# Sorting the rows for the experts by native fp32 products, in two halves with the first experts between them

## The chip, the cores and the metric

The kernel runs on one core of a Trainium2 chip, as one launch. The core has five engines: PE (TensorE, products), DVE (VectorE), ACT (ScalarE), POOL (GpSimd) and SP (SyncE, which here only issues transfers), and 16 DMA engines. They run their own instruction streams and meet at semaphores. The metric is the device time of one execution in microseconds, lower is better.

## The reference

One layer of a hybrid decoder for a prompt of 256 tokens and 8 sequences of 8 tokens, 320 rows of 1024 in all: two attention-like branches, a merge, and a mixture of experts. The change lies in the last part:

```python
t = rmsnorm(x, norm2_g)                       # 320 rows x 1024
g_idx = top-1 of 4 groups;  e_idx, e_p = top-2 of the 8 experts of that group
for each of 32 experts e (w_gate, w_up: 1024 x 256, w_down: 256 x 1024):
    h = silu(t @ w_gate[e]) * (t @ w_up[e])   # for the rows that chose e
    out += (h * combine[:, e]) @ w_down[e]
y = x + out
```

Each row chooses two experts, so there are 640 pairs (slots). All is float32. The weights of the experts are 96 arrays of 1 MB.

## The kernel before, in words

Each engine has one block of code with its instructions in a fixed order; nothing is scheduled by a program. In the order of time:

- The dense part: 48 chunks of weights of 1 MB (`w_dense`), each split by ACT and DVE into a rounded high and a low half (type fp32r, tensor `rm`), and multiplied by PE.
- The router: x1 (the rows after the merge) is scaled to h2 by ACT (L1041). PE makes the logits, and a long chain of small DVE instructions (L1516 to L1547) finds each row's two experts and with them its two places among the 640 slots, sorted by expert.
- The sort: DVE writes a one-hot matrix `onehot` (320 rows in 3 tiles, 640 columns; L1551, L1552), and PE multiplies h2 by it, so that the result `xs` has each slot's row as a column, slots in the order of experts. fp32r products are exact only for rounded data, so h2 goes in as a high part (ACT, L1042) and a low one (POOL, L694, h2 minus the high part). There are 16 pieces (8 blocks of 128 features, two halves of 320 slots) of 5 products each (L2023), in the banks 0 to 3, taken to `xs` by ACT (L1053) and DVE (L1564).
- The experts: POOL (ACT for expert 0) copies the 64 slots from where an expert's begin into `pack`; `gate_up` makes 16 products for gate and up (L2042, L2044), ACT and DVE make `hact`, PE transposes it (L2053), and `down` (L2062) multiplies it by the third array. `start(v + 1)` stands ahead of `down` of v, with v's transposes in its middle. The results go out to `y_rows` by an indirect DMA from POOL (L714). The table of rows that this needs (`rows_ready`) comes from 6 small products (L2081) behind expert 0's gate and up. An expert with more than 64 rows would send all through another path (`crowd`), which isn't taken with these inputs.
- At the end SP reads back x1 and the rows, DVE adds them (L1641), and SP writes y.

The 96 arrays are numbered in the order of use: 0 and 1 are gate and up of expert 0, 2 and 3 those of expert 1, 4 is down of 0, 5 and 6 gate and up of 2, and so on (`unit`). They go through 21 slots of 1 MB, array n in slot n mod 21. SP issues them in this order (L455), and each wait holds all behind it. Waits: 4 and 5 for the dense part's last sections, 6 for the merge's splits, 9 and 10 for the last two chunks to be split, 11 for PE's last dense product, 14 for POOL's subtractions (`h2_split`), 17 for the whole sort (`sorted_full`), and from 21 on for `e_used`, which PE raises twice at the end of `gate_up` and once at the end of `down`.

Of the kernel before, what the change touches and what calls it, by code (L numbers as in the profile page):

```python
# [157 lines left out]
def hybrid_step(nc, A, O):  # L158
# [10 lines left out]
    with ctx:  # L169
# [80 lines left out]
        for i in range(2):  # L250
# [41 lines left out]
        top[0] = base_att  # L292
# [22 lines left out]
        top[0] = base_yrow  # L315
# [10 lines left out]
        assert top[0] <= FW  # L326
        squares, lgT = em[:, 12288 + 384:12288 + 384 + CW], em[:, 12288 + 640:13312]
        turn40 = fm[:, base_masks + 1240:base_masks + 1280]
        blkf = cube(fm[:, base_rt:base_rt + NE * JB], NE)

        top[0] = base_raw + 5 * UN
        xe = cube(take(3 * D), 3)
        gat = [take(D) for _ in range(6)]
        crowd_s = [take(D)[0:NS, :] for _ in range(2)]
        assert top[0] <= base_yrow
# [4 lines left out]
                for i in range(2)]  # L340
# [7 lines left out]
        slot = rawm[8:12] + [halves[8192], halves[8192 + UN], rawm[2], rawm[3], rawm[4], rawm[0], rawm[1],  # L348
                             halves[13312], halves[13312 + UN], halves[13312 + 2 * UN]] + rawm[5:8] + \
                            [halves[q * UN] for q in range(4)]  # L350
        NEARLY = 4
        NSLOT = len(slot)
        pack = [cube(em[:, 12288 + 512 * i:12288 + 512 * (i + 1)], KC) for i in range(2)]
        h2s = [cube(rm[:, 3072 * i:3072 * (i + 1)], 3) for i in range(2)]
        onehot = cube(rm[:, 6144:6144 + 3 * SLOTS], 3)
# [52 lines left out]

        def weights(v, j):

            n = unit(v, j)
            return slot[n % NSLOT]
# [24 lines left out]
        def _(sp):  # L437
# [14 lines left out]
            def load(n):  # L452

                v, j = order[n]
                sp.dma_start(slot[n % NSLOT], A["w_moe"][3 * v + j]).then_inc(landed(v, j)[0], 16)  # L455
# [26 lines left out]
            for n in range(NEARLY, 3 * NE):  # L482
                if n == 4:

                    sp.wait_ge(sem("unit_full"), units(first("out"))[0])
                elif n == 6:

                    sp.wait_ge(sem("m_split"), KC)
                    sp.wait_ge(sem("samp_hi"), 1 + KC)
                elif n in (9, 10):  # L490

                    sp.wait_ge(sem("split_done"), NCH - 1 + n - 9)
                elif n == 11:

                    sp.wait_ge(sem("unit_full"), sum(units(NCH - 1)))
                elif n == 14:

                    sp.wait_ge(sem("h2T_full"), 2 * CPS)
                    sp.wait_ge(sem("h2_split"), 3)
                elif n == 17:  # L500

                    sp.wait_ge(sem("sorted_full"), 2 * KC)
                elif n >= NSLOT:

                    sp.wait_ge(sem("e_used"), n - NSLOT + 1 if n < 3 * NE - 1 else unit(NE - 8, 2) + 1)
                load(n)

            sp.wait_ge(sem("e_used"), 3 * NE - NSLOT + 4)
# [38 lines left out]
        def _(pool):  # L547
# [143 lines left out]
            for t in range(3):  # L691
                r = ROWS[t]
                pool.wait_ge(sem("h2_hi"), t + 1)
                g(nc.gpsimd.tensor_tensor(h2s[1][:, t, :] if t < 2 else h2s[0][NS:2 * NS, t, :], h2[0:r, t, :],  # L694
                                          h2s[0][0:r, t, :], ALU.subtract), sem("h2_split"))

            def packed(v):

                place = pool.value_load(off_i[:, v:v + 1], min_val=0, max_val=SLOTS)
                if v >= 2:  # L700

                    pool.wait_ge(sem("e_used"), unit(v - 2, 1) + 1)
                nc.gpsimd.tensor_copy(pack[v % 2], xs[:, :, bass.ds(place, CAP)]).then_inc(sem("e_packed"), 1)
# [56 lines left out]
        def _(act):  # L760
# [278 lines left out]
            for t in range(3):  # L1039
                r = ROWS[t]  # L1040
                s(A_(h2[0:r, t, :], h2[0:r, t, :], ACT.Copy, scale=small[0:r, 9 + t:10 + t]))  # L1041
                s(A_(h2s[0][0:r, t, :], h2[0:r, t, :], ACT.Copy), sem("h2_hi"))  # L1042
# [7 lines left out]
            for n in range(0, 2 * KC, 2):  # L1050
                k, half = n // 2, n % 2
                act.wait_ge(sem("sorted_full"), n + 1)
                s(A_(xs[:, k, NT * half:NT * (half + 1)], bank[n % 4][:, 0:NT], ACT.Copy), sem("sorted_free_a"))  # L1053
# [8 lines left out]
            act.wait_ge(sem("sorted_free_v"), KC)  # L1062
            A_(pack[0], xs[:, :, 0:CAP], ACT.Copy).then_inc(sem("e_packed"), 1)
            for v in range(NE):

                act.wait_ge(sem("e_used"), unit(v, 1) + 1)
                A_(act_g[v % 2][CAP:2 * CAP, :], bank[v % 2][0:CAP, 0:FE], ACT.Silu).then_inc(sem("e_silu"), 1)  # L1067
                if v >= 1:
                    take_y(v - 1)
            take_y(NE - 1)  # L1070
# [13 lines left out]
        def _(dve):  # L1084
# [464 lines left out]
            s(CP(place[NS:2 * NS, 2, :], place[0:NS, 2, :]))  # L1549
            for t in range(3):  # L1550
                s(TSC(onehot[:, t, :], iota, place[:, t, 0:1], None, ALU.is_equal))  # L1551
                s(STT(onehot[:, t, :], iota, place[:, t, 1:2], onehot[:, t, :], ALU.is_equal, ALU.add),  # L1552
                  sem("onehot"))
# [4 lines left out]
            s(v.tensor_reduce(most[:, 0:1], bank[4][:, 0:NE], AX_X, ALU.max))  # L1558
            dve.wait_ge(sem("x1_stored"), 16)
            s(v.memset(xs[:, :, SLOTS:XC], 0.0))  # L1560
            for n in range(1, 2 * KC, 2):
                k, half = n // 2, n % 2
                dve.wait_ge(sem("sorted_full"), n + 1)
                s(CP(xs[:, k, NT * half:NT * (half + 1)], bank[n % 4][:, 0:NT]), sem("sorted_free_v"))  # L1564
            dve.wait_ge(sem("sorted_free_a"), KC)
            s(v.memset(small[0:1, 94:95], 0.0), sem("xs_ready"))

            for k in range(2):
                s(TT(esel, hot[k], offs.unsqueeze(1).broadcast_to([P, 3, NE]), ALU.mult))
                s(v.tensor_reduce(scal[3 * k + 1], esel, AX_X, ALU.add))  # L1570
                s(TT(scal[3 * k], place[:, :, k], scal[3 * k + 1], ALU.subtract))
                for t in range(3):
                    i, r = 3 * k + t, ROWS[t]
                    s(TSC(at_rank[i][0:r, :], iota[0:r, 0:CAP], scal[3 * k][0:r, t:t + 1], row_of[0:r, i:i + 1],
                          ALU.is_equal, ALU.mult), sem("onehot"))
            dve.wait_ge(sem("router_full"), 6)
            s(TSC(row_i, bank[6][0:CAP, 0:NE], float(NO_ROW), None, ALU.add), sem("rows_ready"))

            def late_words():

                dve.wait_ge(sem("router_exps"), 1)
                s(v.tensor_reduce(wsum, gexp, AX_X, ALU.add))
                s(TSC(wden, second, 1.0, None, ALU.add))
                s(TT(wsum, wsum, wden, ALU.mult))
                s(v.reciprocal(wts[:, :, 0], wsum))
                s(TT(wts[:, :, 1], wts[:, :, 0], second, ALU.mult))
                crowd3 = crowd_i.rearrange("p (t k) -> p t k", t=3)
                for k in range(2):
                    s(STT(crowd3[:, :, k], picks[:, :, k], float(JB * CAP), scal[3 * k], ALU.mult, ALU.add))
                s(CP(flag_i, most[0:1, 0:1]))  # L1590
                for j in range(JB):
                    s(TSC(blkf[0:1, :, j], offs[0:1, :], float(CAP * j), float(SLOTS), ALU.add, ALU.min))
                s(CP(blk_i, blkf[0:1, :, :].rearrange("p e j -> p (e j)")))
# [8 lines left out]
            for e in range(NE):  # L1602
# [4 lines left out]
                if e == 0:  # L1607
                    late_words()
                if e >= 1:
                    take_y(e - 1)  # L1610
                dve.wait_ge(sem("e_hT_full"), e + 1)
                CP(htp[e % 2], cube(bank[2 + e % 2][:, 0:2 * CAP], 2)).then_inc(sem("e_hT"), 1)  # L1612
            take_y(NE - 1)
# [32 lines left out]
        def _(pe):  # L1646
# [372 lines left out]
            def sort(n, t):  # L2019

                k, half = n // 2, n % 2
                for i in range(2 if t < 2 else 1):
                    ins = mm(bank[n % 4][:, 0:NT], h2s[i][:, t, P * k:P * (k + 1)],  # L2023
                             onehot[:, t, NT * half:NT * (half + 1)], start=(t == 0 and i == 0), stop=(t == 2))
# [3 lines left out]
            for t in range(3):  # L2028
                pe.wait_ge(sem("h2_split"), t + 1)
                pe.wait_ge(sem("onehot"), t + 1)  # L2030
                for n in range(4):
                    sort(n, t)
            for n in range(4, 2 * KC):
                pe.wait_ge(sem(("sorted_free_a", "sorted_free_v")[n % 2]), n // 2 - 1)
                for t in range(3):
                    sort(n, t)
# [38 lines left out]

            start(0)
            pe.wait_ge(sem("onehot"), 3 + 6)
            for k in range(2):
                for t in range(3):
                    i, r = 3 * k + t, ROWS[t]  # L2080
                    ins = mm(bank[6][0:CAP, 0:NE], at_rank[i][0:r, :], hot[k][0:r, t, :], start=(i == 0), stop=(i == 5))  # L2081
            ins.then_inc(sem("router_full"), 1)
            for v in range(NE):
# [14 lines left out]
                down(4 + v % 2, htp[v % 2], weights(v, 2)).then_inc(sem("e_used"), 1)  # L2098

# [84 lines left out]
```

## Time and profile before

| what | value |
|---|---|
| three executions | 875.36, 878.8, 879.83 us (median 878.8) |
| the profiled execution | 872.89 us, its span 871.4 us, mean granted clock of PE 0.949 |
| PE busy | 750.2 us, 86% |
| PE's weight loads busy | 597.2 us, 69% |
| DVE busy | 401.8 us, 46% |
| ACT busy | 298.5 us, 34% |
| POOL busy | 144.1 us, 17% |
| DMA | 202.84 MB, mean 233 GB/s |

Busy shares are means over stages that differ. The part at hand begins at about 600 us, where the dense part ends, and goes to the end of the span. A row of a timeline gives start, length, engine, line, operation, operands and the count of instructions merged in it; in square brackets stands how long the engine was idle before it and what ended that. A row of windows gives a stretch, its length, the busy time and instructions of each engine, PE's granted clock (1 is 2.4 GHz, 0.5 is 1.2 GHz), the busy share of the DMA engines and their GB/s.

### The profile page before, as it was taken

The numbers are of one execution on the slowest core, as the hardware profiler recorded it, in microseconds if no ns is written. First come the engines' busy times: TensorE is split into PE (matmuls) and PEld (weight loads), VectorE is DVE, ScalarE is ACT, GpSimd is POOL, SyncE is SP. The second block draws the span as 40 slices with busy tenths as digits, with TensorE's granted clock in tenths as the row PEclk, the third lists the DMA queues.
The fourth block names the chain that finished last, engine by engine and source line by source line (L and its number), as shares of the span: only waits on it lengthen the run. The fifth ranks groups of instructions, "written<-read, shape, count | busy, mean of one in ns | idle before, by whom it ended". The sixth has DMA issues, their size and how long they took to land.

```text
span 871.4 us, 14531 instructions
## 1 busy us (share of the span) xinstructions
PE 750.2 (86%) x5476; PEld 597.2 (69%) x5476; DVE 401.8 (46%) x936; ACT 298.5 (34%) x550; POOL 144.1 (17%) x245
## 2 busy tenths in 40 slices
PE   2999899998888999997968799986589999787780
PEld 1899899996555699996857689985555555444440
DVE  3575333466544456584445547764752222111123
ACT  5433553655333255663221224544221111111110
POOL 5001000002333200103222300001212222112210
PEclk9999999999899999999989999998699999999995
DMA  5245233226677642727565625984579999999986
GB/s 184 97 146 181 101 142 139 104 97 213 173 232 219 194 146 103 255 97 237 140 206 168 191 93 189 347 344 171 224 318 418 417 419 418 419 418 419 418 322 190
DMA packets 38170, 202.84 MB, mean 233 GB/s; under 512 B 7490, under 2 KB 8018, under 8 KB 18898
## 3 DMA queue, kind: packets, MB, share of 16 engines
q1 hardware_dynamic: 24434, 160.29, 48.1%
q0 software_dynamic: 13664, 41.58, 15.3%
q8 instruction: 46, 0.75, 0.4%
q14 instruction: 26, 0.21, 0.1%
HBM read 184.24 MB, written 23.38 MB: 238 GB/s over the span
## 4 chain that ended last, share of the span: by engine, by line
PE 59%; DMA 17%; DVE 11%; ACT 5%; issue 5%; SPq 1%; POOLq 1%; POOL 1%; DVEq 0%; ACTq 0%
PE bank L1694 20%; PE bank L1698 9%; DMA fm<-in_w_moe 7%; DMA em<-in_w_moe 7%; PE bank L2042 6%; PE bank L1684 3%; PE bank L1850 3%; PE bank L2062 3%; DMA fm<-in_cache_lf 2%; DVE rm L1104 2%; PE bank L1899 2%; ACT rm L781 2%; PE bank L2023 2%; PE bank L1839 1%; PE bank L1934 1%
## 5 line engine op out<-in xcount | busy, mean ns | idle before, releaser
L1694 PE MATMUL bank<-rm 128*128 128x320 f32 x1344 | 207.5, 313 | 2.6 <-ACT fm L809 1.6
L1694 PEld LDWEIGHTS bank<-rm 128*128 128x128 f32 x1344 | 199.0, 189 | 7.4 <-issue 3.9
L1104 DVE TENSOR_TENSOR rm<-fm,rm 128x2048 fp32r<-128x2048 f32 x48 | 110.0, 2293 | 69.5 <-ACT rm L781 69.0
L1698 PE MATMUL bank<-rm 128*128 128x256 f32 x960 | 122.4, 286 | 2.4 <-DVE fm L1474 2.4
L1698 PEld LDWEIGHTS bank<-rm 128*128 128x128 f32 x960 | 118.4, 194 | 3.2 <-issue 2.9
L2044 PE MATMUL bank<-fm,em 128*64 128x256 f32 x384 | 98.1, 401 | 0.0
L781 ACT ACTIVATE rm<-fm 128x2048 fp32r<-128x2048 f32 x48 | 91.9, 1915 | 17.8 <-PE bank L1694 11.2
L2042 PE MATMUL bank<-em 128*64 128x256 f32 x272 | 66.7, 389 | 9.8 <-DMA fm<-in_w_moe 6.4
L2042 PE MATMUL bank<-fm,em 128*64 128x256 f32 x240 | 61.7, 404 | 12.2 <-DMA fm<-in_w_moe 10.8
L2042 PEld LDWEIGHTS bank<-em 128*64 128x64 f32 x272 | 35.6, 138 | 36.5 <-issue 21.9
L1067 ACT ACTIVATE fm<-bank 64x256 f32<-64x256 f32 x32 | 12.0, 376 | 136.3 <-PE bank L2044 136.3
L2042 PEld LDWEIGHTS bank<-fm,em 128*64 128x64 f32 x240 | 32.6, 143 | 36.3 <-issue 21.8
L714 POOL DMA_INDIRECT y_rows<-fm,im x32 | 29.3, 915 | 161.5 <-DVE fm L1600 150.5
L2044 PEld LDWEIGHTS bank<-fm,em 128*64 128x64 f32 x384 | 51.7, 142 | 0.0
L1316 DVE SCALAR_TENSOR_TENSOR fm<-fm,bank 128x257 f32<-128x257 f32 x64 | 28.0, 479 | 48.1 <-PE bank L1850 48.1
L648 POOL DMA_DIRECT2D fm<-in_state_C x32 | 17.7, 552 | 178.2 <-DVE fm L1257 118.7
L1684 PE MATMUL bank<-rm 128*128 128x256 f32 x320 | 43.1, 287 | 0.6 <-DVE fm L1445 0.6
L1605 DVE TENSOR_TENSOR fm<-bank,fm 64x256 f32<-64x256 f32 x32 | 13.6, 426 | 63.6 <-ACT fm L1067 63.3
L1684 PEld LDWEIGHTS bank<-rm 128*128 128x128 f32 x320 | 40.0, 191 | 2.8 <-DVE fm L1474 1.5
L1612 DVE COPY fm<-bank 128x128 f32<-128x128 f32 x32 | 9.3, 292 | 66.3 <-PE bank L2053 51.5
L1850 PE MATMUL bank<-fm 64*128 64x257 f32 x128 | 29.6, 471 | 8.1 <-ACT fm L929 7.1
L1600 DVE COPY fm<-bank 64x512 f32<-64x512 f32 x32 | 22.2, 694 | 29.4 <-PE bank L2062 29.4
(387 smaller groups left out, 1013.3 us busy)
## 6 DMA issues: line engine op xcount, KB each, us to landing
fm<-in_w_moe SPq DMA_DIRECT2D x57, 1024.0 KB, 27.6
fm<-in_w_dense SPq DMA_DIRECT2D x48, 1024.0 KB, 4.9
em<-in_w_moe SPq DMA_DIRECT2D x39, 1024.0 KB, 27.7
fm<-in_state_C POOLq DMA_DIRECT2D x32, 257.0 KB, 4.4
out_C_sample<-fm POOLq DMA_DIRECT2D x32, 257.0 KB, 5.3
fm<-in_cache_kT POOLq DMA_DIRECT2D x16, 512.0 KB, 5.0
fm<-in_cache_v POOLq DMA_DIRECT2D x16, 512.0 KB, 4.5
fm<-y_rows SPq DMA_DIRECT2D x4, 512.0 KB, 5.3
```

The lines of the kernel that those rows point to most:

```text
L714: pool.indirect_dma_start(y_rows, bass.IndirectOffsetOnAxis(ap=row_i[:, v:v + 1].bitcast(U32), axis=0), yrow[v % NY], None, bounds_check=6 ...
L781: s(A_(pair[c % 2][0], cube(raw[c % RAW1], KC), ACT.Copy), sem("hi_done"))
L1104: s(TT(pair[c % 2][1], cube(raw[c % RAW1], KC), pair[c % 2][0], ALU.subtract), sem("split_done"))
L1316: done(STT(Cout[n % NCOUT][:, k, :], Cin[n % NCIN][:, k, :], dec8[:, HM * b + h:HM * b + h + 1], bank[bk][:, 0:DE], ALU.mult, ALU.add), bk)
L1600: CP(yrow[v % NY][:, D // 2:D], bank[4 + v % 2][CAP:2 * CAP, :]).then_inc(sem("e_y_right"), 1)
L1684: ins = mm(bank[b][:, 0:CW], samp[:, k, :], w[:, k, :], start=(k == 0 and i == 0), stop=(k == KC - 1 and i == 1))
L1694: ins = mm(bank[b][:, 0:NT], w[:, k, P * u:P * (u + 1)], a[:, k, :], start=first, stop=final)
L1698: ins = mm(bank[b][0:r, 0:CW], a[:, k, TILE0[u]:TILE0[u] + r], w[:, k, :], start=first, stop=final)
L1850: full(mm(bank[bk][:, 0:DE], kwm[n % 2][rows, 0:P], vx2[rows, h, :], start=True, stop=True), bk)
L2042: last_g = mm(bank[b][0:CAP, 0:FE], x[:, k, :], g[:, k, :], start=(k == 0), stop=(k == KC - 1), skip_group_check=True)
L2044: last_u = mm(bank[b][CAP:2 * CAP, 0:FE], x[:, k, :], u[:, k, :], start=(k == 0), stop=(k == KC - 1), skip_group_check=True)
L2062: ins = mm(bank[b][CAP * j:CAP * (j + 1), :], hT[:, k, :], w[:, k, 512 * j:512 * (j + 1)], start=(k == 0), stop=(k == 1), skip_group_check ...
```

## The change

- h2 is sorted as it is: the sort's products take h2 and `onehot` in float32, one product for a tile instead of two. ACT's rounded copy and POOL's subtraction are gone, and PE waits for the scaling alone (`h2_scaled`).
- The slots are sorted in two halves of 320. The first half (8 pieces of 3 products) is done ahead of expert 0. The first five experts can't reach beyond slot 320 (5 x 64; the starts of 1 to 4 are limited to that), so the second half comes later: 4 pieces behind down of expert 1 and 4 behind down of expert 2, in the banks 6 and 7. POOL waits for it ahead of expert 5's pack.
- DVE writes the first half's one-hot columns for the three tiles ahead of the sort, the second's between its evacuations. The table of rows is made behind down of expert 0, some small words later than before.
- Since `rm` holds neither h2's parts nor `onehot`, and h2 lies elsewhere, 18 arrays (0 to 17) have a slot ahead of the sort. 18 to 25 go into the slots of 0 to 7 again, each once its array is used. 26, 27 and 28 take the last three slots, which hold h2 and `onehot` until then, and wait for the whole sort.

```diff
-        slot = rawm[8:12] + [halves[8192], halves[8192 + UN], rawm[2], rawm[3], rawm[4], rawm[0], rawm[1], ...
+        slot = rawm[8:12] + [halves[8192], halves[8192 + UN]] + rawm[2:6] + [rawm[0], rawm[1], halves[13312], ...
...
+        NSLOT, NFREE, NAGAIN = len(slot), 18, 8
+        HALF, NBEFORE = SLOTS // 2, 5
-        h2s = [cube(rm[:, 3072 * i:3072 * (i + 1)], 3) for i in range(2)]
-        onehot = cube(rm[:, 6144:6144 + 3 * SLOTS], 3)
+        onehot = cube(em[:, 0:3 * SLOTS], 3)
...
+        def slot_of(n):
+            if n < NFREE:
+                return n
+            if n < NFREE + NAGAIN:
+                return n - NFREE
+            return n - NAGAIN if n < NSLOT + NAGAIN else slot_of(n - NSLOT)
...
-                elif n in (9, 10):
-                    sp.wait_ge(sem("split_done"), NCH - 1 + n - 9)
-                elif n == 11:
+                elif n in (10, 11):
+                    sp.wait_ge(sem("split_done"), NCH - 1 + n - 10)
+                elif n == 12:
                     sp.wait_ge(sem("unit_full"), sum(units(NCH - 1)))
-                elif n == 14:
-                    sp.wait_ge(sem("h2T_full"), 2 * CPS)
-                    sp.wait_ge(sem("h2_split"), 3)
-                elif n == 17:
+                elif n == NFREE + NAGAIN:
                     sp.wait_ge(sem("sorted_full"), 2 * KC)
-                elif n >= NSLOT:
+                    sp.wait_ge(sem("late_done"), 1)
+                elif NFREE <= n < NFREE + NAGAIN:
+                    sp.wait_ge(sem("e_used"), n - NFREE + 1)
+                elif n >= NSLOT + NAGAIN:
                     sp.wait_ge(sem("e_used"), n - NSLOT + 1 ...
...
-            for t in range(3):
-                r = ROWS[t]
-                pool.wait_ge(sem("h2_hi"), t + 1)
-                g(nc.gpsimd.tensor_tensor(h2s[1][:, t, :] ..., h2[0:r, t, :], h2s[0][0:r, t, :], ALU.subtract), sem("h2_split"))
             def packed(v):
                 place = pool.value_load(off_i[:, v:v + 1], min_val=0, max_val=SLOTS)
+                if v == NBEFORE:
+                    pool.wait_ge(sem("xs_ready"), 2)
...
+            def hot_slots(t, half):
+                w, r = slice(HALF * half, HALF * (half + 1)), ROWS[t]
+                s(TSC(onehot[0:r, t, w], iota[0:r, w], place[0:r, t, 0:1], None, ALU.is_equal))
+                s(STT(onehot[0:r, t, w], iota[0:r, w], place[0:r, t, 1:2], onehot[0:r, t, w], ALU.is_equal, ALU.add), sem("onehot"))
...
-            def sort(n, t):
-                k, half = n // 2, n % 2
-                for i in range(2 if t < 2 else 1):
-                    ins = mm(bank[n % 4][:, 0:NT], h2s[i][:, t, P * k:P * (k + 1)], onehot[:, t, NT * half:NT * (half + 1)], ...)
+            def sort(b, k, half, t):
+                r = ROWS[t]
+                ins = mm(bank[b][:, 0:HALF], h2[0:r, t, P * k:P * (k + 1)], onehot[0:r, t, HALF * half:HALF * (half + 1)], ...)
...
                 down(4 + v % 2, htp[v % 2], weights(v, 2)).then_inc(sem("e_used"), 1)
+                if v == 0:
+                    row_table()
+                elif v in (1, 2):
+                    sort_more(range(4 * (v - 1), 4 * v))
```

On SP, the issues of the experts' arrays from number 6 on, before (`em` and `fm` are the two tensors that hold the slots; a count at the end is of equal rows):

```order
L455 DMA fm<-in_w_moe 128x2048 [waits samp_hi,m_split]
L455 DMA fm<-in_w_moe 128x2048 x2
L455 DMA fm<-in_w_moe 128x2048 [waits split_done] x2
L455 DMA em<-in_w_moe 128x2048 [waits unit_full]
L455 DMA em<-in_w_moe 128x2048 x2
L455 DMA fm<-in_w_moe 128x2048 [waits h2_split,h2T_full]
L455 DMA fm<-in_w_moe 128x2048 x2
L455 DMA em<-in_w_moe 128x2048 [waits sorted_full]
L455 DMA em<-in_w_moe 128x2048 x3
L455 DMA fm<-in_w_moe 128x2048 [waits e_used] x4
```

and now:

```order
L462 DMA fm<-in_w_moe 128x2048 [waits samp_hi,m_split]
L462 DMA fm<-in_w_moe 128x2048 x3
L462 DMA fm<-in_w_moe 128x2048 [waits split_done] x2
L462 DMA em<-in_w_moe 128x2048 [waits unit_full]
L462 DMA em<-in_w_moe 128x2048 x5
L462 DMA fm<-in_w_moe 128x2048 [waits e_used] x4
L462 DMA em<-in_w_moe 128x2048 [waits e_used] x2
L462 DMA fm<-in_w_moe 128x2048 [waits e_used] x2
L462 DMA fm<-in_w_moe 128x2048 [waits late_done,sorted_full]
L462 DMA em<-in_w_moe 128x2048
L462 DMA fm<-in_w_moe 128x2048
```

The issues behind the last dense product are six instead of three, the three behind POOL's subtractions are gone, eight that wait for e_used come next, and the wait for the sort stands ahead of number 26 instead of 17.

On PE, the part from down of expert 0 to the start of expert 3, now (L2080 and L2082 are gate and up, L2091 the transposes, L2100 down, L2120 the table of rows, L2052 the sort):

```order
L2100 MATMUL bank<-em,fm 64x512 [waits e_hT,e_down_in0]
L2100 MATMUL bank<-em,fm 64x512 x3
L2120 MATMUL bank<-fm 64x32 [waits onehot]
L2120 MATMUL bank<-fm 64x32 x5
L2080 MATMUL bank<-em 64x256 [waits e_gate_up_in2,e_hact,e_packed]
...
L2100 MATMUL bank<-fm 64x512 [waits e_hT,e_down_in1]
L2100 MATMUL bank<-fm 64x512 x3
L2052 MATMUL bank<-em,fm 128x320 [waits onehot]
L2052 MATMUL bank<-em,fm 128x320 x5
L2052 MATMUL bank<-em,fm 128x320 [waits sorted_free_a]
L2052 MATMUL bank<-em,fm 128x320 x2
```

Before, no product of the sort stood behind the first expert; the sort began and ended like this:

```order
L2016 MATMUL bank<-rm 128x32
L2023 MATMUL bank<-rm 128x320 [waits onehot,h2_split]
L2023 MATMUL bank<-rm 128x320 x7
...
L2023 MATMUL bank<-rm 128x320 [waits sorted_free_v]
L2023 MATMUL bank<-rm 128x320 x4
L2042 MATMUL bank<-fm,em 64x256 [waits e_gate_up_in0,e_packed]
```

The same 12 products as behind expert 1 stand behind down of expert 2.

## Rows read from the trace of the kernel before

**Rows 1.** Windows, all engines, behind the sort's start; columns as said above.
```profile
624.00:636.00 12.00, 11.32 (x73) 10.79 (x71) 5.32 (x13) 3.50 (x8) 0.00 (x0) 0.96 0.00 0
640.00:740.00 100.00, 98.03 (x744) 52.95 (x742) 28.06 (x71) 16.81 (x35) 25.49 (x34) 1.00 1.01 418
740.00:840.00 100.00, 80.64 (x538) 41.86 (x534) 18.35 (x39) 12.56 (x26) 19.80 (x26) 0.93 1.01 418
```

**Rows 2.** The chain of waits at the end: start, us, what.
```profile
811.52 29.02 DMA fm<-in_w_moe
...
867.31 0.75 DVE fm L1641
```

**Rows 3.** DMA issues of the page: count, size of one, median us to landing.
```profile
fm<-in_w_moe SPq DMA_DIRECT2D x57, 1024.0 KB, 27.6
```

**Rows 4.** Timeline of SP's issues of experts' arrays.
```profile
565.59 20.52 SPq L455 DMA_DIRECT2D fm<-in_w_moe  x5
600.24 1.28 SPq L455 DMA_DIRECT2D em<-in_w_moe  x3
614.56 1.28 SPq L455 DMA_DIRECT2D fm<-in_w_moe  x3
635.52 1.99 SPq L455 DMA_DIRECT2D em<-in_w_moe  x4
640.56 5.83 SPq L455 DMA_DIRECT2D fm<-in_w_moe  x4
```

**Rows 5.** Timeline of POOL and DVE in the router.
```profile
607.25 7.22 POOL L694 TENSOR_TENSOR rm<-fm,rm 128x1024 fp32r<-128x1024 f32 x3 [4.42 <-ACT rm L1042]
...
608.36 1.28 DVE L1522 CAST fm<-im 128x24 f32<-128x24 uint32 x1
...
609.87 2.24 DVE L1528 SCALAR_TENSOR_TENSOR fm<-fm 128x32 f32<-128x32 f32 x1
...
612.67 1.85 DVE L1528 SCALAR_TENSOR_TENSOR fm<-fm 128x32 f32<-128x32 f32 x1
...
615.08 0.19 DVE L1528 SCALAR_TENSOR_TENSOR fm<-fm 128x32 f32<-128x32 f32 x1
...
615.84 0.18 DVE L1533 CAST fm<-im 128x24 f32<-128x24 uint32 x1
```

**Rows 6.** Timeline of the one-hot columns (DVE) and of the sort (PE).
```profile
619.93 0.55 DVE L1551 TENSOR_SCALAR rm<-fm 128x640 fp32r<-128x640 f32 x1
620.52 0.88 DVE L1552 SCALAR_TENSOR_TENSOR rm<-fm,rm 128x640 fp32r<-128x640 f32 x1
...
621.55 4.70 PE L2023 MATMUL bank<-rm 128*128 128x320 f32 x20 [1.90 <-DVE rm L1552]
...
626.42 9.07 PE L2023 MATMUL bank<-rm 128*128 128x320 f32 x60 [0.17 <-ACT fm L1053]
```

**Rows 7.** Windows of PE alone: stretch, length, busy, granted clock, DMA share, GB/s.
```profile
624.00:625.00 1.00, 1.00 (x6) 0.53 0.00 0
625.00:626.00 1.00, 1.00 (x9) 1.00 0.00 0
```

**Rows 8.** Timeline of native fp32 products of full shape in the dense part.
```profile
149.41 0.59 PE L1807 MATMUL bank<-fm 128*128 128x257 f32 x2
149.63 0.84 PEld L1811 LDWEIGHTS bank<-fm 128*128 128x128 f32 x4
...
149.84 1.03 PE L1811 MATMUL bank<-fm 128*128 128x257 f32 x4
```

**Rows 9.** The chain of waits in the first experts: start, us, what.
```profile
640.53 1.02 PE bank L2081 x12
...
650.59 0.26 PE bank L2053 x2
...
656.17 0.27 PE bank L2053 x2
```

**Rows 10.** Timeline of POOL: the pack of expert 2.
```profile
642.56 0.61 POOL L703 COPY em<-fm 128x512 f32 x1 [4.32 <-DVE im L1577]
```

## What I predict, before the changed kernel has run

> **What bounds the kernel now.** I read the windows first, in stretches around the expert part. From 640 to 740 us and from 740 to 840 us the 16 DMA engines are busy all the time and move 418 GB/s, while TensorE has 98 and then 81 of 100 us; from 624 to 636 us nothing moves at all [rows 1]. So behind the sort the weights of the experts are the bound, and before it there is an idle stretch in which they could have come. The chain of waits says the same from the other end: its last long piece is a weight transfer that lands at 840.54 us, and behind it lies a tail of two experts, the last rows and the output, up to 871.4 us [rows 2]. The tail is not touched.
>
> The rest is a count of transfers. One is 1024 KB [rows 3], so at 418 GB/s it takes 2.51 us; there are 96. SP's issues show when they may start: 11, 12 and 13 (counted from 0) at 600.24 us, 14 to 16 at 614.56, when POOL has the last low half, 17 to 20 at 635.52, when the sort is over, and from 21 on as slots come free, from 640.56 [rows 4]. Thus 17 of 96 have come before 635.52, and 79 follow without a gap: 79 x 2.51 = 198 us, and the 7 us left up to 840.5 are for the rows written meanwhile. **Whatever the change does between 600 and 840 us, the end moves by the idle time of DMA that it adds or takes.**
>
> **The change, part by part.**
> *POOL's subtractions go.* Between 607.25 and 614.47 us POOL subtracts three times (2.4 us each). In the same stretch three of DVE's router instructions take 1.28, 2.24 and 1.85 us; the next of the same forms, with POOL idle, take 0.18 and 0.19 [rows 5]. The last long one ends at 614.52 us and POOL's last at 614.47, the first at 609.64 and POOL's first, at a third of its 7.22 us, at 609.66. I take it that they wait for POOL, and that the chain through the router loses (1.28 - 0.18) + (2.24 - 0.19) + (1.85 - 0.19) = 4.8 us. If the three are long for another reason, nothing is won; bounds 0 and 4.8. ACT's three rounded copies (L1042) go as well, which no one waits for any longer.
>
> *The one-hot columns come in halves, and a copy ahead of them goes.* One tile is 0.55 + 0.88 us of DVE for 640 columns [rows 6]; half of it is 0.72, so 0.7 earlier, and the copy at L1549 is 0.2. TensorE began at 621.55; now 621.55 - 4.8 - 0.7 - 0.2 = 615.8. The second halves lie between the evacuations, whose partner TensorE is 1.6 us per bank away, so I cost them at nothing; without that cover they are 2.2 us.
>
> *80 rounded products become 24, and 24 more later.* Before, 20 products took 4.9 us and 60 took 9.1, the first at a granted clock of about 0.5, which is 1.2 GHz [rows 6, 7]. A native product of 320 columns isn't in the trace. The nearest rows: at L1807 and L1811 a product of 257 columns of the same full shape starts 0.43 us after the one ahead, at the full clock [rows 8]. By columns, 320 / 257 x 0.43 = 0.54 us, and 1.07 at 1.2 GHz. Bounds: 0.151 us (what a rounded one of 320 costs, 9.07 / 60) and 0.75 (0.54 and a weight load of 0.21 that isn't hidden). I take 0.54. The clock rose at some 624.94 us (0.53 over 624 to 625, then 1.00), 3.4 us after the dense work began [rows 7]; with that, 3.2 products by 619.2, and 20.8 x 0.54 = 11.2 behind, so the first half ends at **630.4** (before, all of it at 635.5). DVE has x1_stored to wait for; x1 and the first three transfers at 600.24 shared the engines before, as they do now, and its first use is at some 622 us, so nothing.
>
> *From the first half to the end of the second.* From the end of the sort to the end of expert 0's gate and up it was 640.56 - 635.52 = 5.0 us. A further expert is 656.17 - 650.59 = 5.58 us of TensorE [rows 9]. The table of rows is 1.02. It now stands behind down(0), and POOL packs expert 2 only once rows_ready is there: the copy began 642.56 - 641.55 = 1.0 us after the table and takes 0.61 [rows 9, 10], so TensorE stands 1.6 us, where before that lay beside expert 1. Then expert 2's gate and up, down(1), 12 products (6.44), expert 3's and down(2), 12 products. Sum: 5.0 + 5.58 + 1.02 + 1.62 + 5.58 + 6.44 + 5.58 + 6.44 = 37.3 us, so the second half ends at **667.7**. DVE's late words stand behind its copy for down(1) and are covered by the products; before, down(0) waited for them.
>
> *The transfers.* Number 9 needs no end of splitting and is issued with 6 to 8 while the queue is full; 12 to 17 all go at 600.24. They and x1's 1.5 MB are 19 us of DMA, so 18 have come by some 621, when it goes idle. Numbers 18 to 25 each wait for e_used, the first at 630.4 + 5.0 = 635.4 instead of 635.5 for four at once, the last when down(1) ends at 649.3. They need 8 x 2.51 = 20.1 us and have come at **656**. Number 26 waits for the whole sort, 667.7, and SP's queue stands behind it: 12 us idle in the middle of the stretch that sets the end. Then 70 are left.
>
> *Sum.* Before, 79 from 635.5; now 70 from 667.7: 667.7 - 635.5 - 9 x 2.51 = 32.2 - 22.6 = **+9.6 us**. TensorE isn't the bound instead: 28 experts x 5.58 from 667.7 are done at 824, transfers at 850. Against the profiled execution (872.9, span 871.4) that is 882.5; this execution is the fastest of those shown, and on the median of 878.8 it is **888.4 us**.
>
> **A rule against the rows.** The rows show a weight load of 0.21 us for this kind of data (0.84 for four at L1811) and products 0.43 us apart with it, so it is hidden behind 257 columns [rows 8]. The Trainium skill, TensorE: Matmul & The Clock Gate, section "Weight-path perf modes — Fast Weight Load (FWL) and DoubleRow", says that the fast way of loading weights is off for fp32 input. If its cost came out beside the product, each of the 48 would be dearer by the row's 0.21: that is the fourth rival.
>
> **The rivals.**
> 1. *Not slower: the second half is in place before the 26th transfer is asked for, so DMA never idles there.* For it: the rounded product of 320 columns costs 0.151 us. The end moves by 44.8 products (20.8 and 24), so it decides where the second half ends at 658.1, which is a native product of 0.54 - 9.6 / 44.8 = 0.33 us. At 0.27, half of mine, it ends at 655.6 and the change is 655.6 - 658.1 = -2.5 us: 876.3. Against it: 0.43 us for 257 columns, wherever the trace has them.
> 2. *POOL does not hold DVE.* The 4.8 us stay: 893.2. For it: only three of some fifteen instructions there are long. Against: their ends.
> 3. *The clock stays at 1.2 GHz through the first half*, since only 24 products of one kind stand there behind an idle router: 24 x 1.07 = 25.7 instead of 14.6, so 899.5. Against: it rose in 3.4 us before, in the same place.
> 4. *Weight loads beside the products*: 44.8 x 0.21 = 9.4 us, 897.8.
>
> **How the numbers follow.** Forecast 0.68, rival 1 0.12, rival 2 0.11, rivals 3 and 4 together 0.09. The forecast's own range is 882 to 893: 1.6 less if POOL's wait is hidden, 1.7 either way for the clock's rise, and 2.5 either way for how the three runs lie about their median (875.4 to 879.8). With rival 2 above and part of 1 below, 881 to 897. What can be told from no change here is about 0.5%, 4.4 us: slower is above 883.2, faster below 874.4. Rival 1 gives 0.04 to faster and 0.08 to no change; of the forecast 0.04 falls to no change. Faster 0.04, same 0.12, slower 0.84.
>
> **What would show it.** SP's issue of number 26 some 12 us after number 25's transfer has landed, with DMA share 0 between; two idle stretches of DMA (about 621 to 636, 656 to 668) where there was one of 12 us; DVE's L1528 (now L1537) at 0.19 us; native products 0.54 us apart; a gap of about 1.6 us on TensorE ahead of expert 2; the last weights landing at about 850 us of a profile, the tail 31 us as before. I am wrong if issue 26 comes before 658 us, if products are under 0.33 us, or if DMA has a share under 1 behind 668 us, which would mean that it isn't the bound there.

## The result and the profile after

| | executions | median us | lowest to highest |
|---|---|---|---|
| before | 4 | 879.32 | 875.36 to 880.95 |
| after | 4 | **891.87** | 890.79 to 895.51 |

The ratio is 1.0157, with a 95% interval of 1.0112 to 1.0202: slower by 1.6%. I had said 888.4 us, in a range of 881 to 897. The profiled execution of after took 892.09 us, its span is 890.6 us at a mean granted clock of 0.948. That is 19.2 us over the span of before, while the medians are 12.6 us apart; this is taken up below.

In SP's issues of the experts' arrays (start, us, engine, line, operation, operands, count) of after

```profile
567.89 20.54 SPq L462 DMA_DIRECT2D fm<-in_w_moe  x6
602.56 2.98 SPq L462 DMA_DIRECT2D em<-in_w_moe  x6
640.79 4.67 SPq L462 DMA_DIRECT2D fm<-in_w_moe  x4
646.39 7.02 SPq L462 DMA_DIRECT2D em<-in_w_moe  x2
653.45 23.47 SPq L462 DMA_DIRECT2D fm<-in_w_moe  x3
676.97 0.43 SPq L462 DMA_DIRECT2D em<-in_w_moe  x1
```

12 to 17 go together at 602.56 us, 2.3 us later than the same moment of before [rows 4]. This offset comes from the dense part, whose work the change leaves as it is. What makes it is open: that moment lies between 600.2 and 602.0 us in the three profiles of kernels built on before, and between 602.4 and 604.5 in the eight of kernels built on after. Number 18 is asked for at 640.79. The row at 653.45 is the one to learn from: three issues in 23.47 us. 24 and 25 went at its start, the third is number 26, which stood at the head of SP's queue until the sort was over at 676.57, and went at 676.59 (its issue is the last 0.33 us of the row).

The windows (stretch, length, then busy time of PE, PEld, DVE, ACT and POOL, granted clock, DMA share, GB/s) show what the 16 engines did meanwhile, against one idle stretch of some 12 us in before [rows 1]:

```profile
620.00:624.00 4.00, 4.00 (x10) 2.54 (x9) 0.74 (x4) 0.00 (x0) 0.00 (x0) 0.59 0.98 412
625.50:641.70 16.20, 14.83 (x76) 8.18 (x77) 9.36 (x25) 4.04 (x7) 0.61 (x1) 1.00 0.00 0
642.00:665.00 23.00, 21.38 (x130) 11.11 (x128) 5.60 (x19) 2.81 (x6) 3.75 (x5) 1.00 0.90 366
665.00:671.60 6.60, 6.60 (x34) 3.15 (x34) 1.39 (x3) 1.40 (x3) 0.90 (x1) 1.00 0.01 2
672.30:677.60 5.30, 5.30 (x23) 2.72 (x24) 1.25 (x3) 0.44 (x1) 0.00 (x0) 1.00 0.03 5
680.00:740.00 60.00, 60.00 (x452) 31.86 (x448) 15.23 (x32) 10.63 (x22) 15.46 (x21) 1.00 1.01 418
740.00:840.00 100.00, 83.07 (x572) 43.62 (x571) 19.05 (x41) 12.94 (x27) 21.06 (x28) 0.95 1.01 419
```

DMA idles for 16.2 us, then again for 6.6 and 5.3 us while SP holds number 26; behind the sort its share is 1.01 as before. The chain of waits (start, us, what) of after gives the sort's pieces and the last weights:

```profile
618.37 17.36 PE bank L2052 x48
...
646.35 1.02 PE bank L2120 x12
...
654.77 8.03 PE bank L2052 x24
...
668.54 8.03 PE bank L2052 x24
...
829.54 28.35 DMA fm<-in_w_moe
```

The last weights land at 857.89 us, 17.35 later than in before [rows 2]. Each native product is two records, so x48 is 24 products. In the router, DVE's rows of after, which answer to [rows 5, 6]:

```profile
611.08 0.19 DVE L1537 SCALAR_TENSOR_TENSOR fm<-fm 128x32 f32<-128x32 f32 x1
...
613.34 0.18 DVE L1542 CAST fm<-im 128x24 f32<-128x24 uint32 x1
...
617.25 0.39 DVE L1561 TENSOR_SCALAR em<-fm 128x320 f32<-128x320 f32 x1
617.67 0.55 DVE L1562 SCALAR_TENSOR_TENSOR em<-fm,em 128x320 f32<-128x320 f32 x1
```

With POOL idle none of the chain's instructions is long, and POOL packs expert 2 just behind the table of rows, the stall that I had added:

```profile
648.30 0.61 POOL L706 COPY em<-fm 128x512 f32 x1 [9.86 <-DVE im L1601]
```

### The profile page after: what moved, and what is told of

It reads as the page before. It is cut to its first block, busy times and chain, and to the rows that moved or that the text cites. A ratio compares the mean times of both kernels' runs of the same rounds, so it can differ in the third digit from the quotient of the medians.

```text
span 890.6 us, 14548 instructions
## 1 busy us (share of the span) xinstructions
PE 772.6 (87%) x5492; PEld 603.9 (68%) x5492; DVE 396.8 (45%) x934; ACT 295.3 (33%) x547; POOL 136.4 (15%) x242
## 4 chain that ended last, share of the span: by engine, by line
PE 62%; DMA 17%; DVE 10%; ACT 5%; issue 4%; SPq 1%; POOLq 1%; POOL 1%; DVEq 0%; ACTq 0%
PE bank L1724 20%; PE bank L1728 9%; PE bank L2080 7%; DMA em<-in_w_moe 7%; DMA fm<-in_w_moe 6%; PE bank L2052 4%; PE bank L1714 3%; PE bank L1880 3%; PE bank L2100 3%; DMA fm<-in_cache_lf 2%; PE bank L1929 2%; DVE rm L1113 2%; ACT rm L784 2%; PE bank L1869 1%; PE bank L1964 1%
## 5 line engine op out<-in xcount | busy, mean ns | idle before, releaser
L1724 PE MATMUL bank<-rm 128*128 128x320 f32 x1344 | 209.8, 316 | 1.6 <-ACT fm L812 1.6
L2080 PE MATMUL bank<-fm,em 128*64 128x256 f32 x304 | 75.5, 394 | 12.3 <-DMA em<-in_w_moe 6.2
L2082 PE MATMUL bank<-fm,em 128*64 128x256 f32 x320 | 82.6, 405 | 0.0
L2080 PEld LDWEIGHTS bank<-fm,em 128*64 128x64 f32 x304 | 40.3, 140 | 42.0 <-issue 23.2
L2080 PE MATMUL bank<-em 128*64 128x256 f32 x208 | 52.8, 399 | 13.6 <-DMA fm<-in_w_moe 8.0
L2080 PEld LDWEIGHTS bank<-em 128*64 128x64 f32 x208 | 27.8, 142 | 34.5 <-issue 22.0
L2082 PE MATMUL bank<-em 128*64 128x256 f32 x192 | 46.3, 385 | 0.0
L2082 PEld LDWEIGHTS bank<-fm,em 128*64 128x64 f32 x320 | 43.4, 144 | 0.0
```

The source lines that it names most:

```text
L1724: ins = mm(bank[b][:, 0:NT], w[:, k, P * u:P * (u + 1)], a[:, k, :], start=first, stop=final)
L2080: last_g = mm(bank[b][0:CAP, 0:FE], x[:, k, :], g[:, k, :], start=(k == 0), stop=(k == KC - 1), skip_group_check=True)
L2082: last_u = mm(bank[b][CAP:2 * CAP, 0:FE], x[:, k, :], u[:, k, :], start=(k == 0), stop=(k == KC - 1), skip_group_check=True)
```

## Experiments

My theory: the end moves by DMA's idle time. It is set by when the first expert's arrays are used and by when the whole sort is done, since 26 is asked for only then. The rivals: the price lies in the native products alone, wherever they stand; it lies in the experts as such (PE is the bound); POOL's subtraction is no matter. Two groups of kernels ran, each beside the kernel before on its chip, and one more at the end.

**The two kernels again.** 

> The kernel before, once more, with a profile. Two things are to be told apart. The profiled executions of before and of the changed kernel differ by 19.2 us (872.9 and 892.1), the medians by 12.6. If the execution of before that was profiled was merely a fast one, this one has a span of some 876 to 880 us, and the 12.6 stand. If it is again at about 871, the median of before is what is off, and the change costs more than 12.6. Timed against itself it also shows what this measurement can tell: a ratio within 0.5% of 1.

> The changed kernel once more, so that the others of this chip can be held against it. Both theories: 1.5 to 1.6% above the kernel before, two idle stretches of DMA behind 620 us (some 16 and 12 us), the second half of the sort done 74 us behind the issue of array 12.

Before against itself: 876.85 against 876.93 us, ratio 1.0002 (0.9973 to 1.0031), so 0.3% is what this can tell. After: 892.94 us (6 executions) against 877.02, ratio 1.0173 (1.0133 to 1.0214), so the result holds. The profiles' spans were 872.7 and 891.4 us. Executions of before lie between 871 and 884 us and those of after between 890 and 897; the profiles of before both fell into the lower part. The long executions of before go with a lower granted clock: on the chip with 21 of them, those above the median have a mean of 0.943, the others 0.947. I have no profile of a long one, so where they lose the time, and whether the clock is the cause, stays open, and with it the part of the 19 us that the medians (12.6 and 15.9 us) don't show.

**Equal heights of the tiles.** After's third tile has 64 rows, the first two 128. Beside it products of 320 columns cost more than 0.54 us. Here the third tile is filled up to 128 rows with zeros:

```diff
+            memset(xr[NS:P, 2, :], 0.0)          # pad: on DVE, in the dense part; pad2: on POOL, ahead of its iota
-                w, r = slice(HALF * half, HALF * (half + 1)), ROWS[t]
+                w, r = slice(HALF * half, HALF * (half + 1)), P
...
-                r = ROWS[t]
+                r = P
```

> The changed kernel with the third tile of the sort made 128 rows high instead of 64 (rows 64 to 127 of h2's third tile are set to zero by one more DVE instruction, so nothing is added to any sum). In the trace of the changed kernel, products of the same height follow each other after 0.54 us, and it is 0.20 us more before and behind each product of 64 rows. Theory: the weight load of a product isn't hidden when the height changes; then with equal heights the second half's 12 products take 6.4 us instead of 8.0, the whole sort 5.2 us less (3.2 behind the experts, 2.0 ahead), and the time is about 5 us less, 0.6%. Rival: a native product of 320 columns costs 0.67 us in the mean whatever its height; then 8.0 stays and nothing moves.

> The kernel with 128 rows in the third tile (pad), where DVE's extra memset of 0.9 us in the dense part is replaced by one on POOL ahead of its iota. In pad the sort was 5.7 us shorter, as the theory of the unhidden weight load had it, but the last chunks were split 2 us later, and the first array of the batch at the end of the dense part went out 2 us later. Theory (the memset delayed the splits): that batch goes out some 34.7 us behind the issue of array 6, as in the changed kernel, the sort stays short, and the time is 5 to 6 us under the changed kernel's on this chip, 0.6%. Rival (the 2 us are another draw of the clock in the dense part): the batch is again 36.8 us behind, or it varies between executions, and the time is 3 to 6 us under.

Pad: 888.59 us, ratio 1.0151 (1.0113 to 1.0189); but DVE's memset moved the dense part's last issues back by 2 us, and so I ran pad2: 888.47 us against after's 892.94 on the same chip, ratio to before 1.0102 (1.0063 to 1.0142) where after has 1.0173. The spans are 887.2 and 891.4. The chain of pad2 has

```profile
620.02 15.00 PE bank L2053 x48
...
654.07 6.66 PE bank L2053 x24
...
666.46 6.66 PE bank L2053 x24
```

so four pieces of three products take 6.66 us instead of 8.03. That is 0.34 us a piece, though the third product has now twice the rows. The starts of single records in the trace of after say where it was. Those of one piece lie at 629.62, 630.00, 630.27 and 630.53 us (128 rows) and at 630.90 and 631.27 (64 rows), and the next piece begins at 631.63 and goes on at 632.00 (128 rows again). So records are 0.27 us apart, but 0.36 to 0.38 wherever the height changes, and once more behind the first record of the new height: 0.1 + 0.1 = 0.2 us a change. The 64 rows as such cost nothing: where four products of 64 rows stand in a row (625.27 to 627.26), their records are 0.27 apart from the second on. PEld shows the same as an idle engine ahead of each first load of a height (start, us, engine, line, operation, operands, count, idle before):

```profile
629.62 0.84 PEld L2052 LDWEIGHTS bank<-em,fm 128*128 128x128 f32 x4 [0.44 <-issue]
630.90 0.29 PEld L2052 LDWEIGHTS bank<-em,fm 64*128 64x128 f32 x2 [0.44 <-issue]
631.63 0.30 PEld L2052 LDWEIGHTS bank<-em,fm 128*128 128x128 f32 x2 [0.44 <-issue]
```

It follows that 0.2 us comes out beside the products at each change of height: four pieces have seven changes, 1.4 us, and 8.03 - 6.66 is 1.37. A native product is 0.54 us where nothing changes, as forecast: 12 x 0.54 = 6.5 of 6.66. That what comes out is the weight load is likely from the rows above, but no run varies the load by itself. On the same chip the padding was worth 4.5 us by the medians and 4.2 by the spans.

**POOL's subtractions put back**, with their result read by nobody:

```diff
+            for t in range(3):
+                pool.wait_ge(sem("h2_scaled"), t + 1)
+                g(nc.gpsimd.tensor_tensor(y_area[0:r, :], h2[0:r, t, :], h2[0:r, t, :], ALU.subtract))
```

> The changed kernel with three subtractions on POOL again at the old place, of the same size and count, into memory that no one reads; PE doesn't wait for them. Theory: DVE's three router instructions (a cast and two with two inputs) are held by POOL's, the router gets 4.8 us longer, the sort starts 4.8 us later, and so does everything behind it: about +4.8 us, 0.5%. Rival (the long DVE instructions had another reason, such as ACT's copies at that time): the cast and the other two stay at 0.18 and 0.19 us, and the time stays.

894.21 us, ratio 1.0205 (1.0172 to 1.0238). Against after, with 1.0157 and 1.0173 on other chips, that is 0.3 to 0.5% more, and the intervals overlap, so the time alone doesn't show it; the trace does. In its timeline the chain's instructions are held again, but other ones:

```profile
608.39 5.86 POOL L701 TENSOR_TENSOR fm<-fm 128x1024 f32<-128x1024 f32 x3 [3.33 <-ACT fm L1049]
```
```profile
608.47 0.28 DVE L1530 TENSOR_TENSOR fm<-bank,fm 128x120 f32<-128x120 f32 x1 [1.41 <-PE bank L2028]
608.79 1.63 DVE L1531 TENSOR_TENSOR fm<-fm 128x120 f32<-128x120 f32 x1
...
611.89 0.40 DVE L1536 CAST fm<-im 128x24 f32<-128x24 uint32 x1
...
612.53 1.77 DVE L1542 SCALAR_TENSOR_TENSOR fm<-fm 128x32 f32<-128x32 f32 x1
```

POOL's three take 1.9 us each, taken singly, and end at 610.28, 612.26 and 614.24; DVE's three long ones end at 610.42, 612.29 and 614.30. It lost (1.63 - 0.28) + (0.40 - 0.18) + (1.77 - 0.19) = 3.15 us. The sort began at 621.38 instead of 618.37, 3.0 us later, and ended at 680.16 instead of 676.57; the other 0.6 is a clock that rose later. So POOL holds DVE, and where a held instruction falls against POOL's ends decides how much it loses. The row at 608.47 was not held: one of its inputs is in PSUM, the memory of PE's results (`bank`), where those at 608.79 and 612.53 have both in SBUF, the memory of `fm`, `em`, `rm` and `im`. The Trainium skill, SBUF — State Buffer, section "SBUF: two separate sides", says that the two engines share a pair of ports under an exclusive lock: a POOL instruction, or one of DVE's with two inputs in SBUF (against a POOL instruction that reads SBUF) or in a two-port mode, has it for the whole instruction if it starts first, and the other waits. The rows at 608.47, 608.79 and 612.53 agree; the cast at 611.89 has one input, and no row says in which mode it ran.

**The same from the other side: before without POOL's subtractions.** The wait on them goes too, and the high part of h2 is multiplied in the low one's place, so that y counts it twice.

> The kernel before with POOL's three subtractions left out. The low part of h2 isn't made; PE does the same 80 products with the high part in its place, so y lacks the low part's share. Theory (POOL holds DVE's router instructions for 4.8 us): the cast and the two long ones take 0.18 and 0.19 us, the sort ends 4.8 us earlier behind the dense part, and the time falls by 4.8 us, 0.55%: what the change would have won had it done only this. Arrays 14 to 16 also go out 2 us earlier, which DMA's idle stretch swallows. Rival: no difference in DVE's three, and none in the time.

871.97 us against 877.02, ratio 0.9941 (0.9918 to 0.9963), -5.1 us. DVE's cast and the two long ones take 0.18 and 0.19 us. Its chain has the sort's second part and the last weights as follows; in the second profile of before (span 872.7) they are at 627.48 and 841.70.

```profile
623.72 9.08 PE bank L2018 x60
...
808.88 29.03 DMA fm<-in_w_moe
```

**More arrays ahead of the wait for the sort.** Three arrays more go into slots used already, so SP holds number 29 and not 26:

```diff
-        NSLOT, NFREE, NAGAIN = len(slot), 18, 8
+        NSLOT, NFREE, NAGAIN = len(slot), 18, 11
```

> The changed kernel with one number changed: eleven arrays (18 to 28) instead of eight go into slots that the first experts free, and the three slots that wait for the whole sort come in at number 29 instead of 26. PE's work and order stay. Theory (DMA is the bound and its second idle stretch comes from SP's wait at 26): numbers 26, 27 and 28 are issued at about 666 to 668 us of the profile, ahead of the sort's end at 677, so three transfers of 2.51 us lie in the stretch that was idle: -7.5 us, 0.8%. Rival (the end hangs on when PE is done with the sort and the first experts, PE being the bound behind it): the sort's end stays where it is, so nothing moves.

885.2 us, ratio 1.0101 (1.0068 to 1.0135), span 882.5. The sort is not a bit earlier: it ends 74.1 us behind the issue of number 12, and 74.0 in after. Yet the span is 8.1 us shorter. After didn't run on this chip; over before on its own chip it was 12.6 and 15.9 us, and this kernel is 8.3, so the medians give 4 to 8 us. The windows show that DMA worked where it had idled:

```profile
643.00:666.00 23.00, 21.36 (x128) 11.09 (x124) 5.58 (x18) 2.81 (x6) 3.76 (x5) 1.00 0.91 369
666.00:679.00 13.00, 13.00 (x62) 6.44 (x62) 2.88 (x6) 1.84 (x4) 0.90 (x1) 1.00 0.68 254
```

This is the run that tells the order of issue from the native products as a cause: the 96 transfers and all products are the same.

**The second half in four portions, more arrays ahead.** Pad2, with two pieces behind down of each of experts 0 to 3, and NAGAIN 14, so that number 32 is the first to wait for the sort:

```diff
-        NSLOT, NFREE, NAGAIN = len(slot), 18, 8
+        NSLOT, NFREE, NAGAIN = len(slot), 18, 14
...
-                elif v in (1, 2):
-                    sort_more(range(4 * (v - 1), 4 * v))
+                if v < 4:
+                    sort_more((2 * v, 2 * v + 1))
```

> pad2 with the second half of the sort spread over four experts, two pieces (6 products) behind down of each of 0 to 3 instead of four behind 1 and 2, and with fourteen arrays (18 to 31) in slots that the experts free before the three late slots come in. The table of rows goes to bank 5. Theory (DMA's idle time is what counts, and the second idle stretch comes from SP's wait at 26): the experts free arrays as fast as 2.5 us each while the sort goes on, DMA is busy from the first freed slot on, and only the first idle stretch is left. It then has one array more ahead of that stretch than the kernel before, which ends at the same distance from the dense part, so 2.5 us less than before, less a little for the start: a ratio of 0.995 to 1.000, some 13 us under the changed kernel. Rival (PE is the bound: 12 us more of products in the sort): the ratio stays at 1.008 or more.

877.86 us (12 executions), ratio 0.9998 (0.9973 to 1.0023): as fast as before. How much of it is the portions and how much the arrays no run tells apart. Its windows have one idle stretch and then 99 us at 399 GB/s:

```profile
625.90:640.40 14.50, 13.13 (x74) 8.77 (x74) 9.30 (x25) 4.04 (x7) 0.61 (x1) 1.00 0.00 0
641.00:740.00 99.00, 96.91 (x676) 53.07 (x674) 24.69 (x59) 15.66 (x33) 22.00 (x29) 1.00 0.99 399
```

**Both halves ahead of expert 0.** Pad2 with the whole sort where before has it, and 20 slots free instead of 18:

```diff
+            sort_more(range(KC))
...
-                elif v in (1, 2):
-                    sort_more(range(4 * (v - 1), 4 * v))
```

> The kernel after with its third tile padded to 128 rows (memset on POOL), and with both halves of the sort ahead of expert 0, as in the kernel before: 48 native products in a row, the late words and the copies behind them, 20 slots free before an expert is used instead of 18 (18 and 19 ask for the whole sort). Theory (price of the native products, and DMA idle until the sort is over): the first half took 14.3 us in a padded run, the second takes 24 x 0.54 = 13 us, so the sort that began at 619.9 ends at about 647.1 us, DMA is idle from some 626.5 to 648 us (21 us) and not again, with 18 transfers loaded. The kernel before was idle for 12.5 us with 17 loaded; so +9 - 2.5 = +6 us, about 883 where the kernel before has 877, ratio 1.007, 5 us less than with the halves apart (888.5), since there 14.5 + 5.9 + 3.9 us are idle. Rival 1 (the experts between the halves are a gain, as the place they were given suggests): over 888. Rival 2 (the halves apart cost nothing by themselves): 888, as the padded run.

883.45 us against 877.53 (11 and 15 executions), ratio 1.0068 (1.0039 to 1.0096), span 881.7. Expected were 1.007 and 883. Its chain and its windows:

```profile
619.11 28.79 PE bank L2053 x96
```
```profile
626.30:648.30 22.00, 22.00 (x87) 15.24 (x86) 6.83 (x15) 5.04 (x10) 0.24 (x1) 1.00 0.00 0
649.00:740.00 91.00, 88.66 (x678) 48.09 (x676) 27.31 (x70) 14.88 (x31) 22.01 (x29) 1.00 1.01 414
```

So with the halves together the change costs 6 us, net of what POOL's wait gives back. The halves as after has them, with two experts and a queue that holds in between, cost 5 us more (888.5, if the two chips' medians of before, 0.5 us apart, are taken as equal); spread out, with transfers to spare, they give back those 6 us. No version that computes all of the reference was faster than before.

## Why the prediction was right, point by point

The direction, the mechanism and the place were right, and 888.4 is 3.5 us under the median of 891.87. That it lies so near is in part luck: against the profiled execution the same sum said 882.5, and that of after took 892.09. In the profiles the working can be followed to the end. By its own formula the sum was +9.6 us; with the time at which number 26 was issued, less the offset of 2.3 from the dense part, it is 674.3 - 635.5 - 9 x 2.51 = +16.2. What is left to the 19.2 between the spans is the offset of 2.3, the tail (32.7 us instead of 30.9) and 1.1 us less that the transfers behind took than by 2.51 each.

- *POOL holds DVE for 4.8 us*: right. The chain is short in after, 3.15 us came back with POOL's work, and before gained 5.1 us without it. Rival 2 is out.
- *The one-hot halves at 0.72 us*: 0.39 + 0.55 = 0.94, since half the columns cost more than half the time. With the offset the sort should have begun at 618.1 and began at 618.37.
- *The first half, 14.6 us*: **mis-sized**, it took 17.36. The stretch at the low clock (0.50, which is 1.2 GHz) was 4.9 us and not 3.4; at half the speed that costs (4.9 - 3.4) / 2 = 0.75. That part is of the execution and not of the change: in the second profile of after the stretch was 4.2 us and the half took 17.01. The other 2.0 are nearly all changes of height, nine at 0.2.
- *12 products in 6.44 us, twice*: **mis-sized** by 1.6 each, 8.03. I had taken 320 / 257 x 0.43 from a row of full-shape products one behind the other [rows 8] and gave it to every third product with 64 rows as well. Rival 4 (weight loads beside the products, at 4 to 9% with rival 3) was right in part: about 0.2 us, the size of a load, does come out, but only where the number of rows changes and not at each of the 48. Rival 3 is out, the clock rose.
- *37.3 us from one end of the sort to the other*: 40.8, of which 3.2 are the two pieces. The 1.02 for the table, the 1.6 us stall ahead of expert 2 and 5.58 an expert stand.
- *Number 26 holds SP's queue, 12 us idle*: right: 6.6 and 5.3 us, while the first idle stretch grew by some 4 (16.2 instead of 12); again11, with three transfers more ahead of it, gave back 4 to 8 us. Rival 1 (the sort in time before number 26) is out: a native product had to be under 0.33 us for it.
- *DMA is the bound behind the sort*: right: at 740 to 840 us its share was 1.01 or 1.02 in every profile, where PE had 80 to 88 of 100 us. One sign of being wrong came by its letter, a share under 1 behind 668 us (0.03 at 672.3 to 677.6); the cause was number 26, which went at 676.59 and not at 667.7, and behind it the share is 1.01.

The sum of the two mis-sized terms, 2.8 + 3.2, with 0.3 at the start and 0.3 between the pieces, is the 6.6 us by which 16.2 passes 9.6. That the medians are 12.6 apart and not 19 I did not explain; I had set the forecast from before's median, 6 us over its profile, and after's profile lies at its median.

## What to carry to other kernels

Where a transfer stream is the bound, count the transfers that are in place when it first stops and how long each wait at the head of the issuing queue keeps it stopped: what a change wins by ending a stall on one engine (here 4.8 us) is lost if the next in order waits for later work. Order the issues so that the ones that wait for late work come late, and try late work in shorter portions (spread did both at once and was as fast as before). Before a piece of a matrix product is priced by columns, look whether the tiles in it differ in their number of rows.

## What the runs showed of the hardware

- A native fp32 product of 320 columns takes 0.54 us at the full clock, as two records 0.269 us apart, against 0.151 us for a rounded (fp32r) one. A piece of the sort was 5 rounded products (two parts of h2, the third tile holding both), 5 x 0.151 = 0.76 us, and is now 3 native ones, 1.62.
- A change of the number of rows between two products (128 to 64 or back) costs PE about 0.2 us, half of it ahead of the first record of the new height and half behind it (starts 0.36 to 0.38 us apart instead of 0.27), while products of one height, 128 or 64 rows, follow each other without it. Filling up with zeros to the full height was cheaper.
- TensorE's clock rose from 1.2 to 2.4 GHz between 2.9 us (before without POOL's subtractions) and 6.1 us (POOL's subtractions put back) behind the sort's start, with PE busy from about that start on and small products of the router ahead of it. Two profiles of one kernel differ: 3.4 and 3.7 us for before, 4.9 and 4.2 for after; pad2, spread and the kernel with both halves first, which are alike up to the rise, have 3.7, 5.5 and 5.4. What sets it wasn't tried.
- A POOL subtraction of 128x1024 (1.9 to 2.4 us) holds a DVE instruction with both inputs in SBUF, and a cast of 128x24, until it ends; MAX8, FIND_INDEX8 and an instruction with an input in PSUM ran at their usual 0.16 to 0.28 us beside it.
